# Two attention layers in rounds of two head pairs: where the gate products and the value products stand, on a Trainium2 core bound by TensorE

## What is computed

```python
# even layer: 6 heads with a window of 128 and a sink, 6 heads causal with ALiBi, 4 heads on a memory of 256 rows
# odd layer: 12 heads causal with a forget gate (c = cumsum(log_sigmoid(f))), 4 heads on the memory
s = jnp.einsum('bqhd,bshd->bhqs', q, k) * SCALE + bias      # head size 64
p = jax.nn.softmax(s, axis=-1)
o = jnp.einsum('bhqs,bshd->bqhd', p, v)
y = concatenate(heads) * jax.nn.silu(z)                     # z = h @ w_in[:, z columns]
x = x + y @ w_out
```

## Time and profile before

| | |
|---|---|
| median of 3 runs | 1253.01 us (1251.86 to 1253.73) |
| the profiled execution | 1254.13 us, span 1252.3 us |
| PE busy | 1202.2 us (96%) |
| DVE, ACT, POOL busy | 631.6, 567.5, 131.4 us |
| first logits of layer 0, of layer 1 | at 771.38 and 1082.06 us |

### The profile page before, as it was taken

How to read it: one execution, slowest core, us unless ns; L and a number is a source line. 1 busy time by engine, 2 the same in 40 slices (tenths; PEclk the granted TensorE clock), 3 DMA queues, 4 the chain that set the end, 5 groups by cost and what they waited for, 6 DMA issues and landing times.

```text
span 1252.3 us, 17114 instructions
## 1 busy us (share of the span) xinstructions
PE 1202.2 (96%) x6930; PEld 999.7 (80%) x6930; DVE 631.6 (50%) x1173; ACT 567.5 (45%) x1026; POOL 131.4 (10%) x146
## 2 busy tenths in 40 slices
PE   5999999999999999999998999999889999999998
PEld 4887888888977776888997888676878889877688
DVE  5485423688234435415537664865235654355631
ACT  4433331334345444623435665766126567366620
POOL 1000000000000000000000007222400000522422
PEclk8999999999999999999998999999989999999999
DMA  5223322233321122322523342112213323122121
GB/s 176 94 94 100 102 89 85 96 101 101 102 68 35 34 68 67 105 87 93 185 86 85 100 99 70 35 35 68 79 57 103 98 71 127 52 76 81 39 84 53
DMA packets 119047, 105.78 MB, mean 84 GB/s; under 512 B 17836, under 2 KB 115500, under 8 KB 118968
## 3 DMA queue, kind: packets, MB, share of 16 engines
q1 hardware_dynamic: 117320, 98.46, 25.1%
q10 hardware_dynamic: 1648, 6.23, 1.3%
HBM read 102.55 MB, written 2.12 MB: 84 GB/s over the span
## 4 chain that ended last, share of the span: by engine, by line
PE 91%; DVE 4%; ACT 3%; DMA 1%; issue 1%; DVEq 0%; SPq 0%; ACTq 0%
PE acc L1403 26%; PE acc L1405 25%; PE acc L1404 25%; PE acc L1713 3%; PE aux L1739 3%; PE aux L1557 2%; PE aux L1727 2%; PE aux L1571 1%; ACT whi L589 1%; DVE wlo L919 1%; PE acc L1718 1%; PE aux L1621 0%; PE aux L1620 0%; ACT pr L887 0%; DMA raw<-o_w_mem_kv_dram 0%
## 5 line engine op out<-in xcount | busy, mean ns | idle before, releaser
L1403 PE MATMUL acc<-ht_hi,whi 128*128 128x512 f32 x864 | 354.0, 410 | 8.3 <-DVE wlo L919 4.3
L1405 PE MATMUL acc<-ht_hi,wlo 128*128 128x512 f32 x864 | 338.1, 391 | 0.0
L1404 PE MATMUL acc<-ht_lo,whi 128*128 128x512 f32 x864 | 337.9, 391 | 0.0
L919 DVE TENSOR_TENSOR wlo<-raw,whi 128x2048 fp32r<-128x2048 f32 x71 | 163.3, 2303 | 149.7 <-ACT whi L589 149.7
L1403 PEld LDWEIGHTS acc<-ht_hi,whi 128*128 128x128 f32 x864 | 163.0, 189 | 50.9 <-issue 14.8
L1405 PEld LDWEIGHTS acc<-ht_hi,wlo 128*128 128x128 f32 x864 | 162.7, 188 | 34.8
L1404 PEld LDWEIGHTS acc<-ht_lo,whi 128*128 128x128 f32 x864 | 163.3, 189 | 30.2 <-issue 1.9
L589 ACT ACTIVATE whi<-raw 128x2048 fp32r<-128x2048 f32 x71 | 135.3, 1909 | 61.4 <-DMA raw<-o_w_mem_kv_dram 33.0
L535 POOL TENSOR_SCALAR whi<-raw 128x512 fp32r<-128x512 f32 x64 | 42.8, 669 | 1054.6 <-DMA raw<-e_w_in_dram 767.1
L1403 PE MATMUL acc<-whi,ht_hi 128*128 128x256 f32 x416 | 117.8, 283 | 0.0
L1404 PE MATMUL acc<-wlo,ht_hi 128*128 128x256 f32 x416 | 117.7, 283 | 0.0
(11 more groups left out here) (217 smaller groups left out, 1762.0 us busy)
## 6 DMA issues: line engine op xcount, KB each, us to landing
raw<-w_in_dram SPq DMA_DIRECT2D x72, 512.0 KB, 4.5
raw<-o_w_in_dram SPq DMA_DIRECT2D x28, 512.0 KB, 4.6
raw<-e_w_in_dram SPq DMA_DIRECT2D x18, 512.0 KB, 4.8
raw<-w_proj_pool_dram SPq DMA_DIRECT2D x8, 512.0 KB, 3.9
raw<-w_proj_mlstm_dram SPq DMA_DIRECT2D x8, 512.0 KB, 3.9
raw<-w_out_dram SPq DMA_DIRECT2D x8, 512.0 KB, 3.9
raw<-o_w_out_dram SPq DMA_DIRECT2D x8, 512.0 KB, 5.0
raw<-e_w_in_dram SPq DMA_DIRECT2D x12, 256.0 KB, 4.2
```

Of the source, the lines that this page charges most:

```text
L919: v.tensor_tensor(wlo[:, slot, :], raw[:, slot, :], whi[:, slot, :].bitcast(F32), ALU.subtract).then_inc(w_split, 1)
L1403: mm(out_, w_hi_, x_hi, start=first, stop=False)
L1404: mm(out_, w_hi_, x_lo, start=False, stop=False)
L1405: return mm(out_, w_lo_, x_hi, start=False, stop=last)
```

## The change

The loop now has 16 rounds (`NQ`) of two pairs, A = 2i and B = 2i + 1. PE does both logits, turn(A - 2), two z products, turn(A - 1), two z products, and then weighted(A - 2) and weighted(A - 1). The logits have all four banks of `acc`; z has one bank, `aux[2]`, and the output one, `aux[3]`, so that a z half waits for the gate of the half before it, and the first value product of a tile for L1366 of the tile before it. The query blocks of a tile go in the order 0, 3, 1, 2. ACT and DVE have the same instructions as before, in another order. Lines of it, cut to the core:

```diff
-        def logit_bank(e):
-            return acc[:, 2 + e, :]
+        def logit_bank(p, e):
+            return acc[:, 2 * (p % 2) + e, :]
         def trans_bank(e):
             return aux[:, e, :]
-        def out_bank(j):
-            return aux[:, 2 + j % 2, :]
+        z_bank = aux[:, 2, :]
+        out_bank = aux[:, 3, :]
+        ROW_TILES = (0, 3, 1, 2)
...
-            for t in range(TT):
+            for t in ROW_TILES:
...
-        def z_due(p):
-            return p // 4 - 1 if p >= 4 and p % 4 == 0 and p // 4 <= KT else None
+        NQ = NP // 2
+        def z_due(i):
+            return i // 2 - 1 if i >= 2 and i % 2 == 0 and i // 2 <= KT else None
+        def out_due(i):
+            return (i - 3) // 2 if i >= 3 and i % 2 and (i - 3) // 2 < KT else None
...
+                for i in range(NQ + 2):
...
+                    if z_due(i) is not None:
+                        hu = z_due(i)
+                        act.wait_ge(acc_ready, 2 * az + hu + 1)
+                        if hu >= 2:
+                            act.wait_ge(lo_ready, 32 + 8 * L + hu - 1)
+                        nc.scalar.activation(zT[:, hu % 2, :], z_bank, ACT.Tanh, scale=0.5).then_inc(th_ready, 1)
+                    if 1 <= i <= NQ:
+                        normalised(2 * i - 1)
+                    if i < NQ:
+                        probabilities_of(2 * i)
+                    if out_due(i) is not None:
+                        j = out_due(i)
+                        head(zT[:, j % 2, :], op_hi[:, j, :])
+                    if i < NQ:
+                        normalised(2 * i)
+                        probabilities_of(2 * i + 1)
...
+                def gate(hu):
+                    dve.wait_ge(th_ready, 8 * L + hu + 1)
+                    tile = zT[:, hu % 2, :]
+                    ins = v.scalar_tensor_tensor(tile, tile, 1.0, z_bank, ALU.add, ALU.mult)
+                    if hu % 2 == 0:
+                        ins.then_inc(z_half, 1)
+                    else:
+                        if hu == 1:
+                            dve.wait_ge(acc_free, az)
+                        ins.then_inc(acc_free, 1)
+                def gated_out(j):
+                    dve.wait_ge(o_ready, done + TT * (j + 1))
+                    if j % 2:
+                        dve.wait_ge(acc_free, az + j // 2 + 1)
+                    else:
+                        dve.wait_ge(z_half, 4 * L + j // 2 + 1)
+                    tile_written(v.scalar_tensor_tensor(zT[:, j % 2, :], out_bank, 0.5, zT[:, j % 2, :],
+                                                        ALU.mult, ALU.mult))
...
+                for i in range(NQ + 2):
+                    A, B = 2 * i, 2 * i + 1
+                    if 1 <= i <= NQ:
+                        reciprocals(A - 1)
+                    if out_due(i) is not None:
+                        gated_out(out_due(i))
+                    if i < NQ:
+                        if i % 2 == 0:
+                            head_biases(A)
+                        if pairs[A][0].bias is None:
+                            least_of_pair(A)
+                        else:
+                            biased(A, 0)
+                    if z_due(i) is not None:
+                        gate(z_due(i))
+                    if i < NQ and pairs[A][0].bias is not None:
+                        biased(A, 1)
+                    if 1 <= i <= NQ:
+                        turned(A - 2)
+                    if i < NQ:
+                        reciprocals(A)
+                        if pairs[B][0].bias is None:
+                            least_of_pair(B)
+                        else:
+                            biased(B, 0)
+                    if 1 <= i <= NQ:
+                        turned(A - 1)
+                    if i < NQ and pairs[B][0].bias is not None:
+                        biased(B, 1)
+                    if out_due(i) is not None:
+                        j = out_due(i)
+                        rest(zT[:, j % 2, :], op_hi[:, j, :], op_lo[:, j, :])
...
-                            pe.wait_ge(z_half, 4 * L + u)
-                    if k == 0 and half and u:
-                        pe.wait_ge(acc_free, a)
+                            pe.wait_ge(acc_free, a)
+                    if k == 0 and half:
+                        pe.wait_ge(z_half, 4 * L + u + 1)
                     c = k * UC + half * P
-                    ins = product(acc[:, half, :], whi[:, n % SLOTS, c:c + P], wlo[:, n % SLOTS, c:c + P],
+                    ins = product(z_bank, whi[:, n % SLOTS, c:c + P], wlo[:, n % SLOTS, c:c + P],
...
-                    if p:
-                        pe.wait_ge(nm_ready if pairs[p - 1][0].bias is not None else pr_ready, 2 * (done + p))
+                    if p >= 2:
+                        pe.wait_ge(nm_ready if pairs[p - 2][0].bias is not None else pr_ready, 2 * (done + p - 1))
...
-                    if job.t == 0 and (L or j >= 2):
-                        pe.wait_ge(t_ready, 31 + 8 * L + j)
+                    if job.t == 0 and (L or j):
+                        pe.wait_ge(t_ready, 32 + 8 * L + j)
...
-                for p in range(NP + 3):
-                    if p < NP:
-                        logits(p)
-                        z_product(2 * p)
-                    if 2 <= p < NP + 2:
-                        turn(p - 2)
-                    if p < NP:
-                        z_product(2 * p + 1)
-                    elif p < NP + 2:
-                        if p == NP:
-                            pe.wait_ge(acc_free, a_out)
-                            pe.wait_ge(pr_ready, 2 * (done + NP))
-                        first = 3 * (p - NP)
-                        rows_as_tiles_come(n_out, a_out, n_out % SLOTS, a_out % 2, op_hi, op_lo, 32 + 8 * L,
-                                           range(first, first + 3))
-                    if p >= 3:
-                        weighted(p - 3)
+                for i in range(NQ + 1):
+                    if i < NQ:
+                        logits(2 * i)
+                        logits(2 * i + 1)
+                    if 1 <= i <= NQ:
+                        turn(2 * i - 2)
+                    if i < NQ:
+                        z_product(4 * i)
+                        z_product(4 * i + 1)
+                    if i == NQ:
+                        pe.wait_ge(acc_free, a_out)
+                        pe.wait_ge(pr_ready, 2 * (done + NP))
+                        rows_as_tiles_come(n_out, a_out, n_out % SLOTS, a_out % 2, op_hi, op_lo, 32 + 8 * L, range(0, 3))
+                    if 1 <= i <= NQ:
+                        turn(2 * i - 1)
+                    if i < NQ:
+                        z_product(4 * i + 2)
+                        z_product(4 * i + 3)
+                    if i == NQ:
+                        rows_as_tiles_come(n_out, a_out, n_out % SLOTS, a_out % 2, op_hi, op_lo, 32 + 8 * L, range(3, 6))
+                    if i:
+                        weighted(2 * i - 2)
+                        weighted(2 * i - 1)```

In the listings below the pieces come from layer 0. On PE, a window pair in the middle of the loop before (`prT` are the transposed probabilities, `pr` the probabilities, `ht` the activations, `whi` and `wlo` the weights):

```order
L1713 MATMUL acc<-qk_e 128x256 [waits nm_ready]
...
L1403 MATMUL acc<-ht_hi,whi 128x512
L1404 MATMUL acc<-ht_lo,whi 128x512
L1405 MATMUL acc<-ht_hi,wlo 128x512
L1727 MATMUL aux<-ident,pr 128x128 [waits norm_ready,prT_copied]
...
L1405 MATMUL acc<-ht_hi,wlo 128x512
L1739 MATMUL aux<-prT_110,v_e 64x128 [waits prT_copied]
...
L1713 MATMUL acc<-qk_e 128x256 [waits nm_ready]
```

180 lines of the change are left out of this document (74 added, 106 removed).

## The result

The changed kernel takes 1241.52 us (median of 5 runs, 1241.27 to 1245.66), the kernel before 1253.01. The ratio is 0.9922 with an interval of 0.9904 to 0.994: 7.5 to 12 us faster. The forecast was 1246, with 1238 to 1253 as its range. The profiled execution took 1241.27 us, 12.9 less than that of before.

A forecast was written before the change was run, and what follows sets the result against it. It took PE, busy 96%, as the bound, with DVE setting the pace for window pairs. Window +3.2, distance −2.8, forget −2.7, memory −2.5 and ends −2.0 make −6.8, say −7: from 1253.01 to 1246 us, range 1238 to 1253.

The forecast's parts named there:

- window stage: Window pairs of layer 0: DVE sets the pace, the stage gets 3.2 us longer, by the bounds 5 shorter to 6 longer.
- forget: Forget rounds of layer 1: 12 rounds save 2.4 us and a wait of 0.3 goes, 2.7 us faster.
- Price of a change of shape: PE pays 0.31 us per logits block and 0.26 per value block; merging saves 0.57 per distance or memory round.
- The single z bank: Even rounds: z waits for the gate before, 2.6 us in memory rounds, 0.6 in distance rounds, nothing with forget heads.
- DVE's cycle with window pairs: DVE needs 13.0 us per four window pairs, where PE would need 11.2; the stage goes at 13.0.
- the way to the first gate: Start of the window pairs: the first gate lets PE on at 13.2 us from the first logits.
- the 1.4 named as a sign: Rounds 2 and 4 of layer 0: PE waiting 1.4 us for the gate would show the forecast right.
- POOL's lock: Window pairs: POOL's work holds up about five of 12 DVE steps, at half of 1.29 us each, costing 2.6 us.
- The ends: End of each layer's loop: PE's wait for the last gate falls from 1.44 to 0.2 us; two layers save 2.0.
- PE at its own pace everywhere: Rival, all rounds: added waits don't come, but for 2.6 us in memory rounds; 16 us faster, 1237; chance 0.15.
- The z bank that stops every even round: Rival, even rounds: the gate's chain holds PE 1.4 us in each; 6.6 us slower, 1260; chance 0.15.
- The unsaved shape: Rival, logits: the fixed 0.31 belongs to each pair's start, not the shape; 4.3 us less gain, 1250; chance 0.13.

The follow-up runs named there:

- experiment 1: Changed kernel with the values of a round's two pairs apart again, pair A - 2's ahead of the last z product: 1255.18 us, ratio 1.0015 to the kernel before.
- experiment 2: Changed kernel with turn(A-2) put between the logits of A and those of B: 1247.94 us, ratio 0.996 to the kernel before.
- experiment 3: Changed kernel with the gate on DVE ahead of pair A's first subtraction: 1240.55 us, ratio 0.99 to the kernel before.
- experiment 4: Changed kernel with DVE's copy of pair A-1 behind both subtractions of pair B: 1241.40 us, ratio 0.9912 to the kernel before.
- experiment 7: Changed kernel with each sink sum as two one-column additions, without a second SBUF tensor: 1244.98 us, ratio 0.9936 to the kernel before.
- experiment 6: Kernel before with only the last tanh on ACT and the last gate on DVE moved ahead of other work: 1250.33 us, ratio 0.9986.
- experiment 5: Changed kernel with both the gate ahead of A's first subtraction and the copy behind B's subtractions: 1240.86 us, ratio 0.9903 to the kernel before.
- experiment 10: Changed kernel with gate first, copy last, pair A's scaling later on ACT and one-column sink sums: 1239.10 us, ratio 0.99 to the kernel before.

## Why the prediction was right, step by step

By z products, rounds and the output product's eighth group the 9.95 us divide as follows (negative is faster). The window stage ends with the z product of round 6, at 40.63 us; the kernel before had done as much work by 38.6, by the prediction's own count. The forget row is the rounds' difference: 11 × 0.235 us, and 0.4 for the one round of two pairs that waited before (8.01 us in place of 7.59). "Ends" runs from the values behind the last z product to that eighth group: 876.42 to 892.38 before and 871.29 to 885.93 after in layer 0, 15.96 and 14.01 us in layer 1. The second and the fourth row are what the first, third and fifth leave of each layer.

| part | forecast | measured |
|---|---|---|
| window stage | +3.2 | +2.0 |
| distance, and memory of layer 0 | −2.8 − 1.25 | −4.2 |
| forget | −2.7 | −3.0 |
| memory of layer 1 | −1.25 | −1.3 |
| ends of two layers | −2.0 | −3.3 |
| beyond | 0 | −0.2 |
| sum | −6.8 | −10.0 |

- **Price of a change of shape.** Right as a mechanism, by experiments 1 and 2. Its size was 0.57 for a round without causal terms; 6.51 to 5.89 is 0.62. With forget heads 0.2 was taken and 7.59 to 7.355 is 0.235. The waits that were to go with it (0.3) came to 0.4. The rule that it quoted from the Trainium skill, "TensorEngine Tiling (Array Packing)", Key Properties, that a change of tiling mode drains TensorE, agrees with both experiments: 0.40 us for one logits block more and 0.36 for one value block more, sizes which only the runs give. Between values and the logits behind them, which are of two tiled shapes (64 columns, then 64 rows), no such price shows: the values of 256 keys take 0.59 us to the next start ahead of logits as ahead of a product (experiment 1), and the logits behind them 0.63, none of it an entry. There the measurement decides, and a count of mode changes by the rule alone would be too high. It was also right on the causal term that keeps both payments: forget rounds changed by 0.05 in experiment 2.
- **The single z bank.** In memory rounds right: 2.16 us from logits to z in round 14 and 2.25 in round 12, 0.68 and 0.77 of wait against 0.65, and experiment 3 took it away. Forget rounds wait for nothing. The gated distance rounds behind round 6 take 6.88 and 6.82 us beside 6.56 for those without a gate, 0.3 each as forecast, but for the reason given there, DVE late, since the gate's place made a difference of 0.2 us in one of them and none in the other (experiment 3), while moving the copy took the first of them to 6.57 (experiment 4).
- **DVE's cycle with window pairs.** 13.0 us was built from single operations without POOL's lock; the z products behind the gates are 12.97 and 12.91 apart, and only 0.05 us of lock falls between them. This was the number on which most hung, and it was right. But the way to the first gate was 13.2 us forecast and 14.75 measured. Three held-up sums stand there, 1.2 us, and PE waits for the late copies (0.69 and 1.01 us) besides. The waits for the gate in rounds 2 and 4 are therefore 2.1 and 1.8 us (3.33 and 3.06 less 1.27) and not the 1.4 named as a sign.
- **POOL's lock.** 2.6 us forecast, the most mis-sized term of the window stage: twice what was there. The sums (L1314) that were held up took 0.43, 0.73, 0.52 and 0.21 us where 0.16 is free, some 1.25 us in all, nearly all of it ahead of the first gate. It is luck where they fall: in the later variants one sum took 1.09. The rule of the Trainium skill, "SBUF — State Buffer", Who interferes with whom, agrees with experiment 7, in which sums with one SBUF tensor were never held up. What the prediction did not see is that the same lock holds the rest (L965) at the end of layer 0:

```profile
884.56 1.31 DVE L965 TENSOR_TENSOR op_lo<-zT,op_hi 128x512 fp32r<-128x512 f32 x1 [0.70 <-ACT op_hi L625]
```

  POOL's L543 runs from 884.05 to 885.33; PE waits 1.18 us for this line, against 0.56 in layer 1, so 0.62 was lost there. Such a held-up rest explains experiment 6 too.
- **The ends.** The mechanism is right (experiment 6), the size too small: the step took "2 × (1.25 − 0.26)". In layer 1 it is 1.95 us: 1.44 of wait, all of it gone; 0.36 for the merged values behind the last z product, which the forecast had booked with the memory rounds; 0.15 unexplained. The 0.26 had been taken off for a merge at the very end that had never been counted in, and 0.2 had been left as a wait that the order of this kernel avoids.
- **The rivals.** PE at its own pace everywhere is refuted by the window stage (PE waits 5 us there). The z bank that stops every even round did so only in the window stage: 3.33, 3.06 and 3.01 us from logits to z, where 1.3 would do for the first two and 1.7 for the third, but 2.0 and 1.95 with distance heads and no wait with forget heads. The mean over the rounds beyond the window stage was well below the 0.85 us from which it decides. The unsaved shape is refuted.

The forecast missed by 4.5 us in the medians. By the table 3.2 of it are terms that were sized wrongly, all to the same side, the ends (1.3) and the window stage (1.2) above all. The rest fits the clock: the executions of the changed kernel with a mean granted clock of 0.993 took 1241.3 to 1241.5 us, those with 0.989 and 0.990 took 1245.7 and 1244.4, and its median is one of the first. That the median before, 1253.01, is of the other kind is likely from its size (0.990 gave 1252.3 to 1254.2, 0.992 and 0.993 gave 1250.6 to 1252.3 when that kernel was timed beside the experiments), but its own clock isn't on record.

**What stays open.** The window cycle isn't fixed at 12.9 us: with the copy last and no sum held up it is 12.25 (experiment 5) where 12.95 stood, and in the other cycles the lock, or in experiment 10 the dearer sums, took this back. Whether a version without both, with the copy last and the sink's sum on ACT, keeps 12.25 in every cycle wasn't tried. Which exponentials or copies close the ring at that pace wasn't measured either.

## What to carry to other kernels

Price a block of small matmuls between two of another shape by its neighbours, not by its length: entering, a fixed part and leaving made 0.36 to 0.40 us of TensorE here, one such block more per round made 10.5 us of this kernel, and merging two blocks saves one whole price, but only if nothing of the other shape stands between them. When a merge forces a double buffer to become single, look where the releasing instruction stands in its engine's queue: 2.9 us came back for moving the gate ahead of one reduction. When an edit wins nothing, look at each cycle by itself before giving the mechanism up: filling VectorE's wait shortened the cycle by 0.7 us where GpSimd stood still, and the gain went where sums with two SBUF inputs ran beside it.

## What the runs showed of the hardware

Two executions of the same instructions were 3 us apart at a point 770 us in; the granted clock of their first 100 us (0.97 and 0.96 against 0.99 and 0.98) accounts for about 2 of them, more than some edits here are worth. Counting from a common event takes that out, but not what the clock does behind it: one stretch of 25 us at 0.93 in place of 1.00 made the untouched piece between the layers longer by up to a microsecond. The two-operand form of a 128x2 sum on VectorE takes 0.16 us free and up to 1.1 with GpSimd at work; two sums of one column each took 0.34 either way. Head tables (L1326 in the changed file, one SBUF tensor and 512 columns, two of them) took 0.87 us in the kernel before and 1.88 in experiment 10 (L1328 there) while GpSimd was at work, so it isn't the two-operand form alone that is held up:

```profile
832.96 1.88 DVE L1328 TENSOR_SCALAR bias_h<-masks 128x512 f32<-128x512 f32 x2
...
832.50 1.59 POOL L543 TENSOR_TENSOR wlo<-raw,whi 128x512 fp32r<-128x512 f32 x1
```
